# Split products whose moving columns and bank are walked from the last column to the first

## The chip, the core and the metric

The kernel runs on one core of one Trainium2 chip. The metric is the time of one execution on the device in microseconds. Three runs of the kernel before gave 3465.7, 3466.33 and 3469.99 us; the median is 3466.33 us.

## What is computed

The reference is a chain of two transformer blocks over one sequence of 512 positions with 1024 channels, in float32.

- The first block has two layers. Each layer is a gated MLP (`silu(a) * b`, 2816 hidden channels), a mixer, and another gated MLP. The mixer joins sparse attention (compressed, selected and windowed keys, 8 heads) with a gated spatial MLP. Each part has an RMS norm before it, modulated by a condition vector.
- The second block has two layers with a condition vector of its own and a second sequence, the context of 256 positions. Its first layer mixes by pooling, the second by attention over context and latents. Each is followed by an MLP with 4096 hidden channels and a squared ReLU.

Most of the work is in products of the form `x @ W`, with `x` of 512 (or 256) positions:

```
def _swiglu(x, w_in, w_out):
    a, b = jnp.split(x @ w_in, 2, axis=-1)
    return (jax.nn.silu(a) * b) @ w_out
```

## The kernel before

Channels lie on the 128 partitions and positions along the free axis. So an activation tile is `[128, 512]` (128 channels, 512 positions), a half is `[128, 256]`, and the context is `[128, 256]`. A product over 1024 channels is a sum over 8 such tiles.

**The split product.** TensorE is fed with float32 values cut to a shorter format (`F32R`). To keep the accuracy, each weight and each activation is held as a high part and a low part: `WH` and `WL`, `nH` and `nL`, `hH` and `hL`. A product is then three matmuls into the same PSUM bank: high weight by high activation, high weight by low activation, low weight by high activation. The weights are the stationary operand, 128 x 128, and the activations are the moving operand, 512 or 256 columns. These triples are written out in ten places:

- `products` (L662 to L664), which most stages use through `slot_pair`: for each of its `nk` channel tiles it waits for the high and the low part of the activations and issues the triple into one bank.
- `wide_halves_pe` (L1039 to L1041) and `wide_pe` (L1083 to L1085): the same for two to four banks at a time, tile by tile.
- `network_end_pe` (L1299 to L1301), `output_end_pe` (L1345 to L1348), `start_pe` (L1430 to L1432), `second_end_pe` (L2483 to L2485), the blocks at L2562 to L2564, `three` of the context's MLP (L2778 to L2780), and the part of the output projection at L3620 to L3622.

**Weights.** A plan (`plan()`) lists every weight slot in the order of use. SyncE's queue loads a slot of up to 1 MB into a raw buffer, ScalarE rounds it to `WH` (L557), and VectorE subtracts to get `WL` (L568). There are four pairs of `WH` and `WL`; a pair is used again when the last matmul of its slot has counted up a semaphore.

**Readers of the banks.** Each group of matmuls counts up one semaphore with its last instruction. ScalarE or VectorE waits for that count, and then reads the bank: an activation function in the MLPs (L1146), a sum with the residual (L1266, L1277) or with an accumulator (L2454). Eight banks are handed around by `take`.

**Other matmuls.** The attention scores and values (L1737, L1776, L3449, L3477), the transposes (L1756, L3461) and the sums over channels (L877, L882) are plain float32 matmuls, without a split. L3477 is one of them with 512 columns.

The order on each engine is written out by hand; where two stages run beside each other, a helper (`weave`) takes steps of both in turn.

Of the kernel before, what the change touches and what calls it, by code (L numbers as in the profile page):

```python
# [14 lines left out]
KT = 8  # L15
S = 512
# [393 lines left out]
def build(nc, A, out):  # L410
# [3 lines left out]
    with ctx:  # L414
# [234 lines left out]

        def products(pe, k, c, nk, to, xs, ready, group, waits):

            hi, lo = view(M.WH, k), view(M.WL, k)
            cc = slice(c * 128, c * 128 + 128)
            pe.wait_ge(*waits)
            for i in range(nk):
                xh, xl = xs(i)
                (h_hi, v_hi), (h_lo, v_lo) = ready(i)
                pe.wait_ge(h_hi, v_hi)  # L660
                pe.wait_ge(h_lo, v_lo)
                pe.q.matmul(to, hi[:, i, cc], xh, start=i == 0, stop=False)  # L662
                pe.q.matmul(to, hi[:, i, cc], xl, start=False, stop=False)  # L663
                t = pe.q.matmul(to, lo[:, i, cc], xh, start=False, stop=i == nk - 1)  # L664
                if i == nk - 1:
                    t.then_inc(*mm.up(*group))

# [351 lines left out]
        def wide_halves_pe(pe, want, n, g, names):  # L1019

            ks = [slot_pe(pe, want) for _ in range(n)]
            per = slots[ks[0]][5] // 128
            to = []
            for name in names:
                b, free = take(*name)
                pe.wait_ge(*free)
                to.append(b)
            nk = slots[ks[0]][3]
            for x, p in enumerate(lat.half):
                h = g + "AB"[x]  # L1030
                for i in range(nk):
                    pe.wait_ge(*a_xhi.to(h, i))
                    pe.wait_ge(*v_xlo.to(h, i))
                    xh, xl = lat.nH[:, i, p.cols], lat.nL[:, i, p.cols]
                    for j, name in enumerate(names):
                        hi, lo = view(M.WH, ks[j // per]), view(M.WL, ks[j // per])
                        cc = slice(j % per * 128, j % per * 128 + 128)
                        d = to[j][:, p.cols]
                        pe.q.matmul(d, hi[:, i, cc], xh, start=x == i == 0, stop=False, skip_group_check=True)  # L1039
                        pe.q.matmul(d, hi[:, i, cc], xl, start=False, stop=False, skip_group_check=True)  # L1040
                        t = pe.q.matmul(d, lo[:, i, cc], xh, start=False, stop=i == nk - 1, skip_group_check=True)  # L1041
                        if x and i == nk - 1:
                            t.then_inc(*mm.up(*name))
                    if x == 0 and i == 2:
                        half_sum_pe(pe, g + "B", lat.half[1])
                    if x == 0 and i == 4:
                        half_spread_pe(pe, g + "B", lat.half[1])
            for k in ks:
                mm.again("slot", k)
# [15 lines left out]
        def wide_pe(pe, want, n, N, xs, ready, names):  # L1065

            ks = [slot_pe(pe, want) for _ in range(n)]
            per = slots[ks[0]][5] // 128
            to = []
            for name in names:  # L1070
                b, free = take(*name)
                pe.wait_ge(*free)
                to.append(b[:, 0:N])
            nk = slots[ks[0]][3]
            for i in range(nk):
                xh, xl = xs(i)
                (h_hi, v_hi), (h_lo, v_lo) = ready(i)
                pe.wait_ge(h_hi, v_hi)
                pe.wait_ge(h_lo, v_lo)
                for j, name in enumerate(names):  # L1080
                    hi, lo = view(M.WH, ks[j // per]), view(M.WL, ks[j // per])
                    cc = slice(j % per * 128, j % per * 128 + 128)
                    pe.q.matmul(to[j], hi[:, i, cc], xh, start=i == 0, stop=False, skip_group_check=True)  # L1083
                    pe.q.matmul(to[j], hi[:, i, cc], xl, start=False, stop=False, skip_group_check=True)
                    t = pe.q.matmul(to[j], lo[:, i, cc], xh, start=False, stop=i == nk - 1, skip_group_check=True)  # L1085
                    if i == nk - 1:
                        t.then_inc(*mm.up(*name))
            for k in ks:
                mm.again("slot", k)
# [192 lines left out]
        def network_end_pe(g):  # L1282
# [4 lines left out]
            def group(pe, x, o):  # L1287
# [4 lines left out]
                for n, (k, cb, ci, f) in enumerate(parts):  # L1292
                    pe.wait_ge(*a_whi.to(k))
                    pe.wait_ge(*v_wlo.to(k))
                    pe.wait_ge(*a_hhi.to(g, ci, f))
                    pe.wait_ge(*v_hlo.to(g, ci, f))
                    hi, lo = view(M.WH, k)[:, f, 128 * cb:128 * cb + 128], view(M.WL, k)[:, f, 128 * cb:128 * cb + 128]
                    xh, xl = M.hH[:, ci % 2, f, c], M.hL[:, ci % 2, f, c]
                    pe.q.matmul(b[:, 0:S // 2], hi, xh, start=n == 0, stop=False)  # L1299
                    pe.q.matmul(b[:, 0:S // 2], hi, xl, start=False, stop=False)  # L1300
                    t = pe.q.matmul(b[:, 0:S // 2], lo, xh, start=False, stop=n == 5)  # L1301
                t.then_inc(*mm.up(g, "O", x, o))
                if x and o == 3:
                    mm.again("slot", k0)
# [5 lines left out]
        def output_end_pe(g):  # L1310
# [18 lines left out]
            def four(pe):  # L1329
# [6 lines left out]
                for part in (range(6), range(6, 8)):  # L1336
                    for o in range(4):
# [4 lines left out]
                        for i in part:  # L1342
                            pe.wait_ge(*a_hhi.to(g, "m", i))
                            pe.wait_ge(*v_hlo.to(g, "m", i))
                            pe.q.matmul(to[o], hi[:, i, cc], M.mH[:, i, c], start=i == 0, stop=False,  # L1345
                                        skip_group_check=True)
                            pe.q.matmul(to[o], hi[:, i, cc], M.mL[:, i, c], start=False, stop=False, skip_group_check=True)
                            t = pe.q.matmul(to[o], lo[:, i, cc], M.mH[:, i, c], start=False, stop=i == 7,  # L1348
                                            skip_group_check=True)
                        if i == 7:  # L1350
                            t.then_inc(*mm.up(g, "O", 0, o))
# [49 lines left out]
        def start_pe(pe):  # L1401
# [19 lines left out]
            def part(i, which):  # L1421
# [3 lines left out]
                for j in which:  # L1425
# [1 line left out]
                    pe.wait_ge(*a_whi.to(k))  # L1427
                    pe.wait_ge(*v_wlo.to(k))
                    hi, lo = view(M.WH, k), view(M.WL, k)
                    pe.q.matmul(to[j][:, :], hi[:, i, cc], xh, start=i == 0, stop=False, skip_group_check=True)  # L1430
                    pe.q.matmul(to[j][:, :], hi[:, i, cc], xl, start=False, stop=False, skip_group_check=True)
                    t = pe.q.matmul(to[j][:, :], lo[:, i, cc], xh, start=False, stop=i == 7, skip_group_check=True)  # L1432
                    if i == 7:
                        t.then_inc(*mm.up(*names[j]))
                        if j % 2:
# [1031 lines left out]
        def second_end_pe(g):  # L2467
# [4 lines left out]
            def parts(pe, x, o, which, to):  # L2472
                c, cb = lat.half[x].cols, slice(o % 4 * 128, o % 4 * 128 + 128)
                for n in which:
# [3 lines left out]
                    for f in range(4):  # L2478
# [1 line left out]
                        pe.wait_ge(*v_hlo.to(g, ci, f))  # L2480
                        hi, lo = view(M.WH, k)[:, f, cb], view(M.WL, k)[:, f, cb]
                        xh, xl = M.hH2[:, ci % 2, f, c], M.hL2[:, ci % 2, f, c]
                        pe.q.matmul(to, hi, xh, start=n == f == 0, stop=False, skip_group_check=True)  # L2483
                        pe.q.matmul(to, hi, xl, start=False, stop=False, skip_group_check=True)
                        t = pe.q.matmul(to, lo, xh, start=False, stop=n == 1 and f == 3, skip_group_check=True)  # L2485
                if which[-1] == 1:
                    t.then_inc(*mm.up(g, "O", x, o))
                if x and o % 4 == 3 and which[-1] == 1:
# [46 lines left out]
        def after_turn_pe(pe, want, post, g, names, last={}):  # L2535
# [6 lines left out]
            def blocks(x, n, hooks):  # L2542
# [9 lines left out]
                for i in range(KT):  # L2552
# [3 lines left out]
                    for k in n:  # L2556
# [2 lines left out]
                        hi, lo = view(M.WH, k0 + k), view(M.WL, k0 + k)  # L2559
                        for j in range(2):  # L2560
                            cc, d = slice(j * 128, j * 128 + 128), to[2 * k + j][:, c]
                            pe.q.matmul(d, hi[:, i, cc], xh, start=x == i == 0, stop=False, skip_group_check=True)  # L2562
                            pe.q.matmul(d, hi[:, i, cc], xl, start=False, stop=False, skip_group_check=True)
                            t = pe.q.matmul(d, lo[:, i, cc], xh, start=False, stop=i == KT - 1, skip_group_check=True)  # L2564
                            if x and i == KT - 1:
                                t.then_inc(*mm.up(*names[2 * k + j]))
                        if x and i == KT - 1:
# [197 lines left out]
        def context_on_pe(pe):  # L2765
# [9 lines left out]

            def three(to, k, i, cc, xh, xl, start, stop):
                hi, lo = view(M.WH, k), view(M.WL, k)
                pe.q.matmul(to, hi[:, i, cc], xh, start=start, stop=False, skip_group_check=True)  # L2778
                pe.q.matmul(to, hi[:, i, cc], xl, start=False, stop=False, skip_group_check=True)  # L2779
                return pe.q.matmul(to, lo[:, i, cc], xh, start=False, stop=stop, skip_group_check=True)  # L2780

            def first(ci, f):

# [823 lines left out]
        def merge_end_pe():  # L3607
# [4 lines left out]
            def part(pe, x, o, tiles, to):  # L3612
# [4 lines left out]
                for i in tiles:  # L3617
                    pe.wait_ge(*a_yhi.to("y2", i))
                    pe.wait_ge(*v_ylo.to("y2", i))
                    pe.q.matmul(to, hi[:, i, cc], lat.nH[:, i, c], start=i == 0, stop=False, skip_group_check=True)  # L3620
                    pe.q.matmul(to, hi[:, i, cc], lat.nL[:, i, c], start=False, stop=False, skip_group_check=True)
                    t = pe.q.matmul(to, lo[:, i, cc], lat.nH[:, i, c], start=False, stop=i == 7, skip_group_check=True)  # L3622
                if tiles[-1] == 7:
                    t.then_inc(*mm.up("wo", "O", x, o))
                    if x and o % 2:
# [321 lines left out]
```

## Time and profile before

| what | before |
|---|---|
| median of 3 runs | 3466.33 us |
| span of the profiled execution, first to last instruction | 3464.7 us |
| TensorE matmul busy | 3413.6 us (99%), 18494 matmuls |
| TensorE weight load busy | 2874.5 us (83%) |
| VectorE busy | 2165.7 us (63%) |
| ScalarE busy | 1318.4 us (38%) |
| mean granted TensorE clock | 0.997 |
| HBM traffic | 130 GB/s over the span |

The profiled execution has no time of its own beside its span; the timed runs lie 1.0 to 5.3 us above it. A matmul's row in the trace lasts longer than the step from its start to the next one's start, because matmuls are pipelined: 390 ns against about 227 ns for 512 columns. So the pace of TensorE is read from the starts in the time line, and the busy share from how little idle time is left.

### The profile page before, as it was taken

What the parts mean: (1) busy time and instruction counts of PE and PEld (TensorE: products, weight loads), DVE (VectorE), ACT (ScalarE), POOL (GpSimd) and SP (SyncE); (2) the same over time, 40 slices, a digit from 0 to 9 for tenths busy, and PEclk for the clock granted to TensorE, in tenths of its full rate; (3) what the DMA queues carried; (4) which work ended last, traced back from release to release, by engine and by line L of the source; (5) the groups of instructions that cost most, each with busy time, mean ns of one, the idle gap of its engine ahead of it and who ended that gap; (6) DMA issues with size and microseconds to landing.
All of it is one profiled execution on the core that took longest, in us unless ns stands there. A gap on an engine that the chain in (4) does not pass through costs nothing.

```text
span 3464.7 us, 46915 instructions
## 1 busy us (share of the span) xinstructions
PE 3413.6 (99%) x18494; PEld 2874.5 (83%) x18494; DVE 2165.7 (63%) x3570; ACT 1318.4 (38%) x1951; POOL 298.0 (9%) x376
## 2 busy tenths in 40 slices
PE   9999999999999999999999999999999999999998
PEld 7888967898888988896789888899988898588888
DVE  7555565656555655666577777888776556655444
ACT  4222463333222422245333523355533236643222
POOL 0000232001000100023100000012100001210000
PEclk9999999999999999999999999999999999999999
DMA  7444302434444344320243444344444311013221
GB/s 279 188 158 163 107 24 101 163 129 168 158 162 151 134 169 158 148 106 12 101 164 140 149 150 170 146 147 182 172 174 165 117 66 68 25 50 112 96 98 48
DMA packets 85561, 452.01 MB, mean 130 GB/s; under 512 B 10304, under 2 KB 12544, under 8 KB 48608
## 3 DMA queue, kind: packets, MB, share of 16 engines
q1 hardware_dynamic: 83168, 439.10, 34.2%
q0 software_dynamic: 2176, 9.92, 0.8%
q8 instruction: 148, 2.42, 0.3%
q14 instruction: 69, 0.57, 0.0%
HBM read 446.88 MB, written 2.10 MB: 130 GB/s over the span
## 4 chain that ended last, share of the span: by engine, by line
PE 84%; DVE 7%; ACT 3%; issue 2%; DMA 2%; POOL 0%; SPq 0%; DVEq 0%; ACTq 0%; POOLq 0%
PE ps L662 21%; PE ps L663 21%; PE ps L664 21%; DVE WL L568 2%; DMA araw<-in_ast 2%; PE ps L2778 1%; PE ps L2780 1%; PE ps L2779 1%; PE ps L3477 1%; PE ps L1039 1%; PE ps L1040 1%; PE ps L1041 1%; ACT P L1859 1%; PE ps L1776 1%; PE ps L1299 1%
## 5 line engine op out<-in xcount | busy, mean ns | idle before, releaser
L662 PE MATMUL ps<-nH,WH 128*128 128x512 f32 x2256 | 880.3, 390 | 0.4 <-ACT rot L3207 0.4
L664 PE MATMUL ps<-nH,WL 128*128 128x512 f32 x2256 | 877.8, 389 | 0.0
L663 PE MATMUL ps<-nL,WH 128*128 128x512 f32 x2256 | 877.8, 389 | 0.0
L568 DVE TENSOR_TENSOR WL<-raw,WH 128x2048 fp32r<-128x2048 f32 (+2 forms) x297 | 651.6, 2199 | 361.5 <-ACT WH L557 360.0
L557 ACT ACTIVATE WH<-raw 128x2048 fp32r<-128x2048 f32 (+2 forms) x299 | 543.2, 1822 | 561.1 <-PE ps L664 479.9
L662 PEld LDWEIGHTS ps<-nH,WH 128*128 128x128 f32 x2256 | 423.5, 188 | 90.6 <-issue 3.3
L664 PEld LDWEIGHTS ps<-nH,WL 128*128 128x128 f32 x2256 | 423.4, 188 | 88.3
L663 PEld LDWEIGHTS ps<-nL,WH 128*128 128x128 f32 x2256 | 423.5, 188 | 87.2 <-issue 0.2
L628 DVE SCALAR_TENSOR_TENSOR araw<-araw,cB 128x1024 f32<-128x1024 f32 x224 | 275.6, 1230 | 205.6 <-DMA araw<-in_ast 205.2
L662 PE MATMUL ps<-hH,WH 128*128 128x512 f32 x944 | 368.8, 391 | 2.5 <-DVE ma L2454 1.4
L664 PE MATMUL ps<-hH,WL 128*128 128x512 f32 x944 | 367.4, 389 | 0.0
L663 PE MATMUL ps<-hL,WH 128*128 128x512 f32 x944 | 367.2, 389 | 0.0
L1146 ACT ACTIVATE scr<-ps 128x512 f32<-128x512 f32 x152 | 89.5, 595 | 414.4 <-PE ps L664 387.2
L1012 POOL TENSOR_SCALAR scr<-scr,der,mods 128x256 f32<-128x256 f32 x112 | 86.2, 771 | 1805.8 <-DVE scr L925 1804.8
L1153 ACT ACTIVATE hH<-scr 128x512 fp32r<-128x512 f32 x152 | 95.8, 633 | 357.5 <-DVE scr L1199 355.5
L662 PEld LDWEIGHTS ps<-hH,WH 128*128 128x128 f32 x944 | 177.2, 188 | 40.3 <-DVE ma L2454 1.9
L664 PEld LDWEIGHTS ps<-hH,WL 128*128 128x128 f32 x944 | 177.2, 188 | 36.9
L663 PEld LDWEIGHTS ps<-hL,WH 128*128 128x128 f32 x944 | 177.2, 188 | 36.6
L1199 DVE TENSOR_TENSOR scr<-scr,ps 128x512 f32<-128x512 f32 x88 | 59.5, 687 | 108.4 <-PE ps L664 107.0
L1266 DVE SCALAR_TENSOR_TENSOR h<-ps,der,h 128x512 f32<-128x512 f32 x144 | 99.7, 746 | 27.2 <-PE ps L664 25.9
L1202 DVE TENSOR_TENSOR scr<-scr 128x512 f32<-128x512 f32 x64 | 43.1, 690 | 101.3 <-ACT scr L1146 100.9
L1208 DVE TENSOR_TENSOR hL<-scr,hH 128x512 fp32r<-128x512 f32 x152 | 100.8, 687 | 4.3
(452 smaller groups left out, 5940.0 us busy)
## 6 DMA issues: line engine op xcount, KB each, us to landing
raw<-in_wst SPq DMA_DIRECT2D x273, 1024.0 KB, 4.8
araw<-in_ast SPq DMA_DIRECT2D x225, 512.0 KB, 5.7
raw<-in_wst SPq DMA_DIRECT2D x18, 512.0 KB, 3.3
araw<-in_wst SPq DMA_DIRECT2D x9, 1024.0 KB, 4.8
row<-in_ast SPq DMA_DIRECT2D x15, 512.0 KB, 10.5
cw<-in_cw POOLq DMA_DIRECT2D x4, 1024.0 KB, 5.9
h<-in_xT SPq DMA_DIRECT2D x4, 512.0 KB, 5.6
raw<-in_wst SPq DMA_DIRECT2D x8, 256.0 KB, 2.6
```

The source lines that it names most:

```text
L557: act.q.activation(M.WH[k % NW][:, 0:n], M.raw[raw_use[k]][:, 0:n], ACT.Copy).then_inc(*a_whi.up(k))
L568: dve.q.tensor_tensor(M.WL[k % NW][:, 0:n], M.raw[raw_use[k]][:, 0:n], M.WH[k % NW][:, 0:n].bitcast(F32), ALU.subtract).then_inc(*v_wlo.up(k))
L628: dve.q.scalar_tensor_tensor(out=w[:, :], in0=w[:, :], scalar=1.0, in1=M.cB[q][:, :], op0=ALU.mult, op1=ALU.mult, accum_out=total).then_in ...
L662: pe.q.matmul(to, hi[:, i, cc], xh, start=i == 0, stop=False)
L663: pe.q.matmul(to, hi[:, i, cc], xl, start=False, stop=False)
L664: t = pe.q.matmul(to, lo[:, i, cc], xh, start=False, stop=i == nk - 1)
L1012: pool.q.tensor_scalar(p.scr[2 + i % 2][:, p.cols], p.scr[i % 2][:, p.cols], G[:, i:i + 1], shift[:, i:i + 1], ALU.mult, ALU.add).then_inc ...
L1146: act.q.activation(p.scr[n % 2][:, 0:N], bank(g, "a", ci, f)[:, 0:N], ACT.Silu if gated else ACT.Relu).then_inc(*empties(a_fn, g, "a", ci, f))
L1153: act.q.activation(hH[:, ci % 2, f, :], p.scr[(2 if gated else 0) + f % 2][:, 0:N], ACT.Copy if gated else ACT.Square).then_inc(*a_hhi.up( ...
L1199: dve.q.tensor_tensor(p.scr[2 + u][:, 0:N], p.scr[u][:, 0:N], bank(g, "b", ci, f)[:, 0:N], ALU.mult).then_inc(*empties(v_pr, g, "b", ci, f))
L1208: dve.q.tensor_tensor(hL[:, ci % 2, f, :], p.scr[2 + f % 2][:, 0:N], hH[:, ci % 2, f, :].bitcast(F32), ALU.subtract).then_inc(*v_hlo.up(g, ...
L1266: dve.q.scalar_tensor_tensor(out=M.h[:, o, :], in0=bank(g, "o", ci, o)[:, :], scalar=gate[:, o:o + 1], in1=M.h[:, o, :], op0=ALU.mult, op1 ...
```

## The change

A helper `back(a)` returns `a[:, ::-1]`, the same columns in reverse order. In all ten places, each of the three matmuls of a triple gets its output and its moving operand through `back`. The weights stay as they are. Each column is still multiplied by the same weights and lands in the same place of the bank; the instruction starts with the last column and ends with the first. The other matmuls are not touched, and neither is anything on the other engines. The diff, cut to the helper, the first two places and the context's:

```diff
@@ -649,6 +649,10 @@
 
 
 
+        def back(a):
+
+            return a[:, ::-1]
+
         def products(pe, k, c, nk, to, xs, ready, group, waits):
 
             hi, lo = view(M.WH, k), view(M.WL, k)
@@ -659,9 +663,9 @@
                 (h_hi, v_hi), (h_lo, v_lo) = ready(i)
                 pe.wait_ge(h_hi, v_hi)
                 pe.wait_ge(h_lo, v_lo)
-                pe.q.matmul(to, hi[:, i, cc], xh, start=i == 0, stop=False)
-                pe.q.matmul(to, hi[:, i, cc], xl, start=False, stop=False)
-                t = pe.q.matmul(to, lo[:, i, cc], xh, start=False, stop=i == nk - 1)
+                pe.q.matmul(back(to), hi[:, i, cc], back(xh), start=i == 0, stop=False)
+                pe.q.matmul(back(to), hi[:, i, cc], back(xl), start=False, stop=False)
+                t = pe.q.matmul(back(to), lo[:, i, cc], back(xh), start=False, stop=i == nk - 1)
                 if i == nk - 1:
                     t.then_inc(*mm.up(*group))
 
@@ -1036,9 +1040,9 @@
                         hi, lo = view(M.WH, ks[j // per]), view(M.WL, ks[j // per])
                         cc = slice(j % per * 128, j % per * 128 + 128)
                         d = to[j][:, p.cols]
-                        pe.q.matmul(d, hi[:, i, cc], xh, start=x == i == 0, stop=False, skip_group_check=True)
-                        pe.q.matmul(d, hi[:, i, cc], xl, start=False, stop=False, skip_group_check=True)
-                        t = pe.q.matmul(d, lo[:, i, cc], xh, start=False, stop=i == nk - 1, skip_group_check=True)
+                        pe.q.matmul(back(d), hi[:, i, cc], back(xh), start=x == i == 0, stop=False, skip_group_check=True)
+                        pe.q.matmul(back(d), hi[:, i, cc], back(xl), start=False, stop=False, skip_group_check=True)
+                        t = pe.q.matmul(back(d), lo[:, i, cc], back(xh), start=False, stop=i == nk - 1, skip_group_check=True)
                         if x and i == nk - 1:
                             t.then_inc(*mm.up(*name))
                     if x == 0 and i == 2:
...
@@ -2775,9 +2779,9 @@
 
             def three(to, k, i, cc, xh, xl, start, stop):
                 hi, lo = view(M.WH, k), view(M.WL, k)
-                pe.q.matmul(to, hi[:, i, cc], xh, start=start, stop=False, skip_group_check=True)
-                pe.q.matmul(to, hi[:, i, cc], xl, start=False, stop=False, skip_group_check=True)
-                return pe.q.matmul(to, lo[:, i, cc], xh, start=False, stop=stop, skip_group_check=True)
+                pe.q.matmul(back(to), hi[:, i, cc], back(xh), start=start, stop=False, skip_group_check=True)
+                pe.q.matmul(back(to), hi[:, i, cc], back(xl), start=False, stop=False, skip_group_check=True)
+                return pe.q.matmul(back(to), lo[:, i, cc], back(xh), start=False, stop=stop, skip_group_check=True)
 
             def first(ci, f):
 
...
```

The places left out have the same three lines with the same edit.

## Rows read from the trace of the kernel before

**Rows 1.** The page: its head, TensorE's busy time, and the granted clock in 40 slices.
```profile
span 3464.7 us, 46915 instructions
...
PE 3413.6 (99%) x18494; PEld 2874.5 (83%) x18494; DVE 2165.7 (63%) x3570; ACT 1318.4 (38%) x1951; POOL 298.0 (9%) x376
...
PEclk9999999999999999999999999999999999999999
```

**Rows 2.** The page: chain that ended last, by engine and by line.
```profile
PE 84%; DVE 7%; ACT 3%; issue 2%; DMA 2%; POOL 0%; SPq 0%; DVEq 0%; ACTq 0%; POOLq 0%
PE ps L662 21%; PE ps L663 21%; PE ps L664 21%; DVE WL L568 2%; DMA araw<-in_ast 2%; PE ps L2778 1%; PE ps L2780 1%; PE ps L2779 1%; PE ps L3477 1%; PE ps L1039 1%; PE ps L1040 1%; PE ps L1041 1%; ACT P L1859 1%; PE ps L1776 1%; PE ps L1299 1%
```

**Rows 3.** Waits of TensorE: line, awaited engine and line, us in total, times, longest.
```profile
PE ps L1756 <- ACT P L1859: 9.0, 25, 0.5
```

**Rows 4.** Groups by form: line, tiles, shapes, count | busy us, mean ns | idle before; 512 columns.
```profile
L662 PE MATMUL ps<-nH,WH 128*128 128x512 f32 x2256 | 880.3, 390 | 0.4 <-ACT rot L3207 0.4
...
L662 PE MATMUL ps<-hH,WH 128*128 128x512 f32 x944 | 368.8, 391 | 2.5 <-DVE ma L2454 1.4 <-DVE h L1266 1.1
...
L662 PE MATMUL ps<-yaH,WH 128*128 128x512 f32 x64 | 24.9, 389 | 0.0
...
L1430 PE MATMUL ps<-nH,WH 128*128 128x512 f32 x48 | 19.0, 397 | 2.4 <-DVE WL L568 1.4 <-DVE nL L1524 0.8 <-PE ps L682 0.2
...
L1083 PE MATMUL ps<-nH,WH 128*128 128x512 f32 x16 | 6.2, 389 | 0.0
```

**Rows 5.** The same view, 256 columns, first line of each triple.
```profile
L1039 PE MATMUL ps<-nH,WH 128*128 128x256 f32 x320 | 92.1, 288 | 0.3
...
L1299 PE MATMUL ps<-hH,WH 128*128 128x256 f32 x288 | 82.7, 287 | 1.0 <-DVE hL L1208 0.6
...
L2483 PE MATMUL ps<-hH,WH 128*128 128x256 f32 x256 | 73.2, 286 | 0.0
...
L2562 PE MATMUL ps<-nH,WH 128*128 128x256 f32 x192 | 57.1, 297 | 3.2 <-DVE nL L930 1.9 <-DVE WL L580 1.1
...
L3620 PE MATMUL ps<-nH,WH 128*128 128x256 f32 x128 | 37.3, 291 | 0.0
...
L1345 PE MATMUL ps<-mH,WH 128*128 128x256 f32 x64 | 18.1, 283 | 0.0
...
L662 PE MATMUL ps<-nHk,WH 128*128 128x256 f32 x32 | 8.9, 279 | 0.0
...
L662 PE MATMUL ps<-nHc,WH 128*128 128x256 f32 x16 | 4.5, 281 | 0.0
```

**Rows 6.** Time line of TensorE, 24 starts apart: start us, duration us, line; 512 columns.
```profile
1000.25 0.39 PE L662 MATMUL ps<-hH,WH 128*128 128x512 f32 x1
...
1005.69 0.39 PE L662 MATMUL ps<-hH,WH 128*128 128x512 f32 x1
```

**Rows 7.** Time line of TensorE, 27 starts apart; 256 columns.
```profile
3417.22 0.28 PE L2484 MATMUL ps<-hL,WH 128*128 128x256 f32 x1
...
3420.46 0.28 PE L2484 MATMUL ps<-hL,WH 128*128 128x256 f32 x1
```

**Rows 8.** Time line of TensorE in the context's MLP, 12 starts apart.
```profile
2381.88 0.28 PE L2778 MATMUL ps<-hHc,WH 128*128 128x256 f32 x1
...
2383.24 0.28 PE L2778 MATMUL ps<-hHc,WH 128*128 128x256 f32 x1
```

**Rows 9.** Time line of TensorE two starts apart, and the window's busy times, clock.
```profile
2865.61 0.41 PE L2564 MATMUL ps<-nH,WL 128*128 128x256 f32 x1
...
2866.04 0.41 PE L2563 MATMUL ps<-nL,WH 128*128 128x256 f32 x1
...
2865.00:2868.00 3.00, 2.98 (x12) 2.80 (x13) 0.97 (x5) 0.00 (x0) 0.00 (x0) 0.50 0.56 194
```

**Rows 10.** Chain in order of time: start us, duration us, what.
```profile
2947.52 5.15 PE ps L3477 x12
```

**Rows 11.** Window from 2300 to 2400 us: busy times in the page's order of engines.
```profile
2300.00:2400.00 100.00, 99.16 (x791) 95.76 (x791) 91.03 (x106) 58.38 (x68) 28.03 (x20) 1.00 0.47 172
```

More of the change, by code:

```diff
@@ L1082, in wide_pe @@
                     cc = slice(j % per * 128, j % per * 128 + 128)
-                    pe.q.matmul(to[j], hi[:, i, cc], xh, start=i == 0, stop=False, skip_group_check=True)
-                    pe.q.matmul(to[j], hi[:, i, cc], xl, start=False, stop=False, skip_group_check=True)
-                    t = pe.q.matmul(to[j], lo[:, i, cc], xh, start=False, stop=i == nk - 1, skip_group_check=True)
+                    pe.q.matmul(back(to[j]), hi[:, i, cc], back(xh), start=i == 0, stop=False, skip_group_check=True)
+                    pe.q.matmul(back(to[j]), hi[:, i, cc], back(xl), start=False, stop=False, skip_group_check=True)
+                    t = pe.q.matmul(back(to[j]), lo[:, i, cc], back(xh), start=False, stop=i == nk - 1, skip_group_check=True)
                     if i == nk - 1:
@@ L1298, in group @@
                     xh, xl = M.hH[:, ci % 2, f, c], M.hL[:, ci % 2, f, c]
-                    pe.q.matmul(b[:, 0:S // 2], hi, xh, start=n == 0, stop=False)
-                    pe.q.matmul(b[:, 0:S // 2], hi, xl, start=False, stop=False)
-                    t = pe.q.matmul(b[:, 0:S // 2], lo, xh, start=False, stop=n == 5)
+                    pe.q.matmul(back(b[:, 0:S // 2]), hi, back(xh), start=n == 0, stop=False)
+                    pe.q.matmul(back(b[:, 0:S // 2]), hi, back(xl), start=False, stop=False)
+                    t = pe.q.matmul(back(b[:, 0:S // 2]), lo, back(xh), start=False, stop=n == 5)
                 t.then_inc(*mm.up(g, "O", x, o))
@@ L1344, in four @@
                             pe.wait_ge(*v_hlo.to(g, "m", i))
-                            pe.q.matmul(to[o], hi[:, i, cc], M.mH[:, i, c], start=i == 0, stop=False,
+                            pe.q.matmul(back(to[o]), hi[:, i, cc], back(M.mH[:, i, c]), start=i == 0, stop=False,
                                         skip_group_check=True)
-                            pe.q.matmul(to[o], hi[:, i, cc], M.mL[:, i, c], start=False, stop=False, skip_group_check=True)
-                            t = pe.q.matmul(to[o], lo[:, i, cc], M.mH[:, i, c], start=False, stop=i == 7,
+                            pe.q.matmul(back(to[o]), hi[:, i, cc], back(M.mL[:, i, c]), start=False, stop=False, skip_group_check=True)
+                            t = pe.q.matmul(back(to[o]), lo[:, i, cc], back(M.mH[:, i, c]), start=False, stop=i == 7,
                                             skip_group_check=True)
@@ L1429, in part @@
                     hi, lo = view(M.WH, k), view(M.WL, k)
-                    pe.q.matmul(to[j][:, :], hi[:, i, cc], xh, start=i == 0, stop=False, skip_group_check=True)
-                    pe.q.matmul(to[j][:, :], hi[:, i, cc], xl, start=False, stop=False, skip_group_check=True)
-                    t = pe.q.matmul(to[j][:, :], lo[:, i, cc], xh, start=False, stop=i == 7, skip_group_check=True)
+                    pe.q.matmul(back(to[j][:, :]), hi[:, i, cc], back(xh), start=i == 0, stop=False, skip_group_check=True)
+                    pe.q.matmul(back(to[j][:, :]), hi[:, i, cc], back(xl), start=False, stop=False, skip_group_check=True)
+                    t = pe.q.matmul(back(to[j][:, :]), lo[:, i, cc], back(xh), start=False, stop=i == 7, skip_group_check=True)
                     if i == 7:
@@ L2482, in parts @@
                         xh, xl = M.hH2[:, ci % 2, f, c], M.hL2[:, ci % 2, f, c]
-                        pe.q.matmul(to, hi, xh, start=n == f == 0, stop=False, skip_group_check=True)
-                        pe.q.matmul(to, hi, xl, start=False, stop=False, skip_group_check=True)
-                        t = pe.q.matmul(to, lo, xh, start=False, stop=n == 1 and f == 3, skip_group_check=True)
+                        pe.q.matmul(back(to), hi, back(xh), start=n == f == 0, stop=False, skip_group_check=True)
+                        pe.q.matmul(back(to), hi, back(xl), start=False, stop=False, skip_group_check=True)
+                        t = pe.q.matmul(back(to), lo, back(xh), start=False, stop=n == 1 and f == 3, skip_group_check=True)
                 if which[-1] == 1:
@@ L2561, in blocks @@
                             cc, d = slice(j * 128, j * 128 + 128), to[2 * k + j][:, c]
-                            pe.q.matmul(d, hi[:, i, cc], xh, start=x == i == 0, stop=False, skip_group_check=True)
-                            pe.q.matmul(d, hi[:, i, cc], xl, start=False, stop=False, skip_group_check=True)
-                            t = pe.q.matmul(d, lo[:, i, cc], xh, start=False, stop=i == KT - 1, skip_group_check=True)
+                            pe.q.matmul(back(d), hi[:, i, cc], back(xh), start=x == i == 0, stop=False, skip_group_check=True)
+                            pe.q.matmul(back(d), hi[:, i, cc], back(xl), start=False, stop=False, skip_group_check=True)
+                            t = pe.q.matmul(back(d), lo[:, i, cc], back(xh), start=False, stop=i == KT - 1, skip_group_check=True)
                             if x and i == KT - 1:
@@ L3619, in part @@
                     pe.wait_ge(*v_ylo.to("y2", i))
-                    pe.q.matmul(to, hi[:, i, cc], lat.nH[:, i, c], start=i == 0, stop=False, skip_group_check=True)
-                    pe.q.matmul(to, hi[:, i, cc], lat.nL[:, i, c], start=False, stop=False, skip_group_check=True)
-                    t = pe.q.matmul(to, lo[:, i, cc], lat.nH[:, i, c], start=False, stop=i == 7, skip_group_check=True)
+                    pe.q.matmul(back(to), hi[:, i, cc], back(lat.nH[:, i, c]), start=i == 0, stop=False, skip_group_check=True)
+                    pe.q.matmul(back(to), hi[:, i, cc], back(lat.nL[:, i, c]), start=False, stop=False, skip_group_check=True)
+                    t = pe.q.matmul(back(to), lo[:, i, cc], back(lat.nH[:, i, c]), start=False, stop=i == 7, skip_group_check=True)
                 if tiles[-1] == 7:
```

## The prediction

> **What bounds the kernel now.** The head of the profile page comes first: the reader is to see a TensorE that is busy for 3413.6 of 3464.7 us, under a granted clock of nine tenths or more in every slice [rows 1]. A busy matmul row says little of pace, though, since each row lasts about 390 ns while the next one starts much earlier. So the second view is the chain of waits by engine and line: 84% of it lies on TensorE, and the three lines of `products` alone make 63% (21% each) [rows 2]. Third, the table of waits: the longest sum of idle time that any producer causes before a matmul line is 9.0 us, and it belongs to transposes that the change leaves alone [rows 3]. The kernel is bound by how fast TensorE takes one matmul after another, and the only question is what this change does to that pace.
>
> The pace stands in the time line. In a run of 512-column split products the starts go from 1000.25 to 1005.69 us over 24 steps, 0.2267 us each [rows 6]. In a run of 256-column ones they go from 3417.22 to 3420.46 us over 27 steps, 0.1200 us each [rows 7]. The difference, 106.7 ns for 256 columns, is 0.4167 ns a column, one column per cycle of the 2.4 GHz level at which the clock stands there. What is left is the same for both widths: 226.7 - 213.3 = 13.3 ns and 120.0 - 106.7 = 13.3 ns, a fixed term for each matmul. A split product therefore costs 0.4167 ns times its columns plus 13.3 ns, and the change can act on either part.
>
> **How many there are.** The 512-column groups come in threes of equal count: 2256 + 944 + 2 x 64 + 48 + 2 x 16 = 3408 triples, or 10,224 matmuls (the rows with 64 and 16 each stand for two groups) [rows 4]. The 256-column ones: 320 + 288 + 3 x 256 + 2 x 192 + 128 + 64 + 32 + 16 = 2000 triples, or 6,000 matmuls (256 stands for three groups, 192 for two) [rows 5]. At the paces above these are 10,224 x 0.2267 = 2318 us and 6,000 x 0.1200 = 720 us, together 3038 us, 88% of the span. All 16,224 are changed, out of 18,494.
>
> **The change part by part.**
>
> *Instructions, waits, queues.* Nothing is added or removed: `back` makes a view, and each matmul keeps its weights, its waits, its place in the order and its increment. The helper writes the same columns to the same places, only in the other order. No DMA is moved, and no wait is added on any engine. Cost 0.
>
> *The readers of the banks and of the moving tiles.* ScalarE and VectorE wait for the increment of the last matmul of a group, not for single columns. The column that is written last is now column 0 instead of 511, and neither end is read earlier. Cost 0. The weight loads stay as they are, with 128 columns read forwards, and they run beside the matmul before. Cost 0.
>
> *Reading the moving columns backwards.* The time line has no matmul that reads with a negative step, so its price has to be bounded. The step keeps its size of one element; the address falls instead of rising. From below: nothing can go faster than one column per cycle, so the column part cannot shrink, and only the fixed term can: at most 13.3 x 16,224 = 216 us. The nearest row of a shorter one is a stretch of context products in which the starts go from 2381.88 to 2383.24 us over 12 steps, 113.3 ns each, 6.7 ns less than usual for 256 columns [rows 8]. From above: the stream falls to half its pace. Two rows show what that costs. The float32 matmuls of L3477 take 5.15 us for 12, 429 ns for 512 columns [rows 10]. In the one stretch where the granted clock is 0.50 (the 1.2 GHz level; TensorE had sat idle before it), 256-column split products start at 2865.61 and 2866.04, two steps in 0.43 us, 215 ns each [rows 9]. I take 0: the nearest rows are those of the same instruction with a step of the same size, and nothing in them suggests that 0.4167 ns a column depends on whether addresses rise.
>
> *Writing the bank backwards.* The same bounds, since one stream feeds the other. Every output slice here has 256 or 512 columns and starts at an even column, so the backward walk starts at an odd one (511, or 255), and it takes neighbours in the same pairs as the forward walk (511 with 510, instead of 510 with 511). If the memory takes columns by twos, no pair is torn. I take 0 again.
>
> Here the Trainium skill has a rule that speaks against the change. The row shows full pace at rising addresses, 0.4167 ns a column [rows 6, 7]; no row shows falling ones. In the Trainium skill, "Advanced Engine Details and Errata", section "PSUM Cachelines", PSUM has lines of 8 bytes, two float32 values, and any access pattern that isn't contiguous slows matmuls down significantly, since every two consecutive elements should be contiguous. By a strict reading, a falling pattern isn't contiguous and the first rival below holds; by the reason that the section gives, each two consecutive elements still share one such line and the cost is 0. I hold with the reason, and no row here decides it.
>
> *Sum.* 0 + 0 + 0 + 0 = 0 against the profiled execution's span of 3464.7 us. The median of the timed runs is 3466.33 us, 1.6 us above that span; the forecast is **3466.3 us**.
>
> **Rivals.**
>
> *A: the stream falls to half pace (slower).* Place: the two-column step at the read or at the bank write. If hardware merges two columns into one access only when addresses rise, each column takes its own, and the matmul goes at the pace of rows 9 and 10. Price: 10,224 x (0.429 - 0.2267) = 2068 us and 6,000 x (0.215 - 0.120) = 570 us, so 3466 + 2638 = about **6100 us**. For it speaks that the float32 matmuls of the same width go at just that pace [rows 10], so a slower mode of the stream exists and a column isn't bound to 0.4167 ns. Against it: in those the slower pace goes with the number format, not with an order of columns. It decides as soon as one of the two sides can't merge falling pairs.
>
> *B: the fixed term gets longer (slower).* Place: the seam between two matmuls, where the reader now has to begin at the far end of a row, and the first columns come later. If the seam is paid twice, the price is another 13.3 ns x 16,224 = 216 us, **3682 us**; each nanosecond is 16.2 us, and it shows from 0.43 ns a matmul. For it: a fixed term exists at full clock and is not explained by the column count [rows 6, 7]. Against it: it is the same for 256 and 512 columns, so it looks like a property of the switch and not of where a row begins.
>
> *C: the fixed term gets shorter (faster).* The same seam in the other direction. The row at 113.3 ns shows that 6.7 ns of it can go, without any change in the instructions [rows 8]. If all split products went that way: 6.7 x 16,224 = 108 us, **3358 us**. What is late next is then VectorE, which is busy for 91% of the stretch from 2300 to 2400 us [rows 11]; there the gain would stop at about 9 of 100 us. Elsewhere TensorE has room, as it waits for almost nothing [rows 3]. Against it: that row is a stretch in which reading order was the usual one, so something else brings it about.
>
> *D: the change doesn't do what it says.* The addresses could be put in rising order again on the way to the instruction. Then nothing changes: 3466 us, the same as the forecast, told apart only by the pattern of the instructions.
>
> **How the numbers follow.** Forecast (no change in pace) 0.64, D 0.02, A 0.11, B 0.11, C 0.12. A change of 0.2% (7 us, 0.43 ns a matmul) is about what a measurement of this kernel can tell from none. So faster 0.12, same 0.66, slower 0.22. The forecast's own range is 3460 to 3473 us. A is so far off that it can't be held in a range of use, and with its 0.11 left out, the range takes about half of B and of C: from 3440 (1.6 ns less a matmul: 16.2 x 1.6 = 26) to 3520 us (3.3 ns more a matmul: 54). About 0.11 + 0.05 + 0.05 lies outside.
>
> **What would show it.** In the profile after, the starts in a run of 512-column split products should be 226 to 227 ns apart and those of 256-column ones 120 ns; the mean durations in the groups should stay at 389 to 391 and 280 to 288 ns [rows 4, 5], TensorE's busy time near 3413 us and the granted clock full. 429 and 215 ns would be rival A. A shift that is the same number of nanoseconds for both widths would be B or C; a shift that doubles from 256 to 512 columns would be a change of the stream's pace, and would prove the argument from rows 6 and 7 wrong. If the pace stands and the time still moves, the cause lies in the readers of the banks, which I have put at 0.

## The result: 1.65% slower

Three runs of the changed kernel gave 3523.08, 3524.57 and 3524.7 us, against 3465.7 to 3469.99 us before. The ratio is 1.0165, with a 95% interval of 1.0147 to 1.0183: slower by 58 us. The forecast was 3466.3 us, no change, with a range up to 3520 us; the time lies above it.

The head of the page of the changed kernel, its chain by engine and by line, and the longest wait, which answer to [rows 1 to 3]. The lines of `products` have moved from L662 to L666, because of the new helper.

```profile
span 3522.8 us, 46915 instructions
...
PE 3476.8 (99%) x18494; PEld 2875.3 (82%) x18494; DVE 2167.6 (62%) x3570; ACT 1317.1 (37%) x1951; POOL 297.0 (8%) x376
...
PEclk9999999999999999999999999999999999999999
...
PE 89%; DVE 5%; ACT 3%; issue 1%; DMA 0%; POOL 0%; DVEq 0%; SPq 0%; ACTq 0%; POOLq 0%
```

```profile
PE ps L1760 <- ACT P L1863: 9.2, 26, 0.5
```

The other engines do what they did: VectorE 2167.6 us against 2165.7, ScalarE 1317.1 against 1318.4, the same wait of 9 us, the same clock. TensorE alone is busy for longer, by 63.2 us, and its share of the chain went from 84 to 89%. So the time went into the matmuls.

Which of them is seen in the groups by form (line, tiles, shapes, count, then busy us and mean ns), against [rows 4, 5]:

```profile
L666 PE MATMUL ps<-nH,WH 128*128 128x512 f32 x2256 | 898.7, 398 | 0.4 <-ACT rot L3211 0.4
...
L666 PE MATMUL ps<-hH,WH 128*128 128x512 f32 x944 | 376.3, 399 | 0.7 <-DVE h L1270 0.7
...
L1043 PE MATMUL ps<-nH,WH 128*128 128x256 f32 x320 | 91.7, 286 | 0.5 <-issue 0.2
...
L2487 PE MATMUL ps<-hH,WH 128*128 128x256 f32 x256 | 72.9, 285 | 0.0
```

With 512 columns a matmul's row became 8 ns longer (390 to 398, 391 to 399); with 256 columns it became 1 to 2 ns shorter. The pace is again in the starts of the time line: 24 steps apart at 512 columns and 30 steps apart at 256.

```profile
1005.05 0.40 PE L666 MATMUL ps<-nH,WH 128*128 128x512 f32 x1
...
1010.65 0.40 PE L666 MATMUL ps<-nH,WH 128*128 128x512 f32 x1
```

```profile
3474.78 0.28 PE L2488 MATMUL ps<-hL,WH 128*128 128x256 f32 x1
...
3478.32 0.28 PE L2488 MATMUL ps<-hL,WH 128*128 128x256 f32 x1
```

That is 5.60 / 24 = 233.3 ns against 226.7 [rows 6], and 3.54 / 30 = 118.0 ns (118.3 from the unrounded starts) against 120.0 [rows 7]. The steps at 256 columns are no longer even: they run 115 to 123 ns in a pattern. At 10,224 matmuls, 6.67 ns would make 68 us. Summed over every step from one start to the next, which takes in the waits, the 512-column split products grew by 63.0 us (2330.8 to 2393.8), those of 256 columns fell by 3.1 us (737.3 to 734.2), and all others by 1.6 us. Together that is 58.3 us, against 58.1 in the span.

### The profile page after: what moved, and what is told of

It reads as the page before. It is cut to its first block, busy times and chain, and to the rows that moved or that the text cites. A ratio compares the mean times of both kernels' runs of the same rounds, so it can differ in the third digit from the quotient of the medians.

```text
span 3522.8 us, 46915 instructions
## 1 busy us (share of the span) xinstructions
PE 3476.8 (99%) x18494; PEld 2875.3 (82%) x18494; DVE 2167.6 (62%) x3570; ACT 1317.1 (37%) x1951; POOL 297.0 (8%) x376
## 4 chain that ended last, share of the span: by engine, by line
PE 89%; DVE 5%; ACT 3%; issue 1%; DMA 0%; POOL 0%; DVEq 0%; SPq 0%; ACTq 0%; POOLq 0%
PE ps L666 22%; PE ps L667 22%; PE ps L668 22%; PE ps L2782 2%; PE ps L2784 2%; PE ps L2783 2%; PE ps L3481 1%; ACT P L1863 1%; PE ps L1043 1%; PE ps L1044 1%; PE ps L1045 1%; PE ps L1780 1%; PE ps L1303 1%; PE ps L1304 1%; PE ps L1305 1%
## 5 line engine op out<-in xcount | busy, mean ns | idle before, releaser
L666 PE MATMUL ps<-nH,WH 128*128 128x512 f32 x2256 | 898.7, 398 | 0.4 <-ACT rot L3211 0.4
L667 PE MATMUL ps<-nL,WH 128*128 128x512 f32 x2256 | 896.5, 397 | 0.0
L668 PE MATMUL ps<-nH,WL 128*128 128x512 f32 x2256 | 896.5, 397 | 0.0
L666 PEld LDWEIGHTS ps<-nH,WH 128*128 128x128 f32 x2256 | 424.2, 188 | 104.3 <-issue 3.3
L666 PE MATMUL ps<-hH,WH 128*128 128x512 f32 x944 | 376.3, 399 | 0.7 <-DVE h L1270 0.7
L667 PE MATMUL ps<-hL,WH 128*128 128x512 f32 x944 | 375.1, 397 | 0.0
L668 PE MATMUL ps<-hH,WL 128*128 128x512 f32 x944 | 375.1, 397 | 0.0
L666 PEld LDWEIGHTS ps<-hH,WH 128*128 128x128 f32 x944 | 177.5, 188 | 43.6 <-DVE h L1270 1.1
```

Source lines behind the costliest of these rows:

```text
L666: pe.q.matmul(back(to), hi[:, i, cc], back(xh), start=i == 0, stop=False)
L667: pe.q.matmul(back(to), hi[:, i, cc], back(xl), start=False, stop=False)
L668: t = pe.q.matmul(back(to), lo[:, i, cc], back(xh), start=False, stop=i == nk - 1)
```

## The experiments

**Read or write (e1, e2), and the width (e3).** The helper was split in two, `back` for the moving operand and `back_out` for the output. In e1 `back` returns `a[:, ::-1]` and `back_out` returns `a`, so only the moving operand is turned round. In e2 it is the other way about. In e3 both are turned round, but only where there are 256 columns. Against the kernel before, cut to one matmul and to e3's helpers:

```diff
-                pe.q.matmul(to, hi[:, i, cc], xh, start=i == 0, stop=False)
+                pe.q.matmul(back_out(to), hi[:, i, cc], back(xh), start=i == 0, stop=False)
...
+        def back(a):
+
+            return a[:, ::-1] if a.shape[1] == S // 2 else a
+
+        def back_out(a):
+
+            return a[:, ::-1] if a.shape[1] == S // 2 else a
```

> All ten places read their moving columns backwards and write the bank forwards, so the columns of every split product land in reverse order (the output is not the reference's). Theory 1 (the read): about 3524 us, as the changed kernel, and 233 ns a 512-column matmul. Theory 2 (the write): about 3466 us and 227 ns.

> All ten places read forwards and write the bank backwards (the output is not the reference's). Theory 1 (the read): about 3466 us and 227 ns. Theory 2 (the write): about 3524 us and 233 ns. If each half costs something, both lie between.

> Only the products of 256 columns (6,000 matmuls) are walked backwards, read and write; those of 512 columns go forwards as before. In the changed kernel the 256-column starts came in a pattern of 115 to 123 ns with a mean near 118.5 in place of 120. Theory 'the term depends on the width': 512-column matmuls at 227 ns, 256-column ones at about 118.5, so 6000 x 1.2 ns = 7 us less than before, about 3459 us. Theory 'the seam costs the same for each': about 6000/16224 of the 58 us lost, 3488 us.

| kernel | median us | ratio to before | 95% interval |
|---|---|---|---|
| e1, read backwards | 3524.18 | 1.0169 | 1.0154 to 1.0184 |
| e2, write backwards | 3465.42 | 0.9998 | 0.9989 to 1.0008 |
| e3, both, 256 columns only | 3459.68 | 0.9984 | 0.9975 to 0.9993 |

The time line of e1 and then that of e2, 24 steps apart each:

```profile
1004.71 0.40 PE L672 MATMUL ps<-nH,WL 128*128 128x512 f32 x1
...
1010.31 0.40 PE L672 MATMUL ps<-nH,WL 128*128 128x512 f32 x1
```

```profile
999.75 0.39 PE L671 MATMUL ps<-nL,WH 128*128 128x512 f32 x1
...
1005.19 0.39 PE L671 MATMUL ps<-hL,WH 128*128 128x512 f32 x1
```

Reading backwards alone gives 233.3 ns and the whole loss. Writing backwards alone gives 226.7 ns and no loss. e3 came out as its first theory said (3459 expected, 3459.68 measured): 256 columns gain a little, and that version is faster than the kernel before by 0.16%. (The 118.5 ns that it was expected to show had been read from the changed kernel.)

**The pace by itself (m1).** A small kernel keeps activations and weights resident and lets TensorE run alone, with one stretch of 48 matmuls for each variant. It ran once, with the granted clock at 1.00 in every stretch.

> A small kernel in place of the whole computation (its output is not the reference's): TensorE alone runs stretches of 48 split-product matmuls on resident tiles, one source line per stretch, with the moving columns, the bank's columns, both or neither walked backwards, for 512, 448, 384, 320 and 256 columns, with the weights taken 4 to 128 columns further on, with 96, 64 or 32 weight columns in place of 128, and in bf16 and plain float32. Theory 1 (the moving read, falling beside a weight load, loses time to it): read-only costs 233.3 ns at 512 columns as both do, write-only stays at 226.7; the fixed term shrinks with the number of weight columns (64 columns: about half of 13.3 ns forward and of 20 ns backward), and shifting the weights changes it. Theory 2 (the bank's write in falling order costs at the seam): write-only costs 233.3, read-only 226.7, and the number of weight columns changes nothing. Either way the plain float32 form should stay at 429 ns, since it runs at half the pace.

One triple of it, as it stands when both operands are turned round (`q` is put here for the shift of the weights, which each stretch has as a number; the triple stands on one line there):

```
mm(back(banks[b][:, 0:512]), hi[:, i, q:q+128], back(nH[:, i, 0:512]), start=i == 0, stop=False)
mm(back(banks[b][:, 0:512]), hi[:, i, q:q+128], back(nL[:, i, 0:512]), start=False, stop=False)
mm(back(banks[b][:, 0:512]), lo[:, i, q:q+128], back(nH[:, i, 0:512]), start=False, stop=i == 7)
```

Its time line, always 24 steps apart: L69 forwards, L71 read backwards, L73 written backwards, L109 forwards with the weights 16 columns on, L117 forwards with them 64 columns on.

```profile
40.71 0.39 PE L69 MATMUL ps<-nH,WL 128*128 128x512 f32 x1
...
46.15 0.39 PE L69 MATMUL ps<-nH,WL 128*128 128x512 f32 x1
...
51.63 0.40 PE L71 MATMUL ps<-nH,WL 128*128 128x512 f32 x1
...
57.23 0.40 PE L71 MATMUL ps<-nH,WL 128*128 128x512 f32 x1
...
62.81 0.39 PE L73 MATMUL ps<-nH,WL 128*128 128x512 f32 x1
...
68.25 0.39 PE L73 MATMUL ps<-nH,WL 128*128 128x512 f32 x1
...
225.18 0.39 PE L109 MATMUL ps<-nH,WL 128*128 128x512 f32 x1
...
230.78 0.39 PE L109 MATMUL ps<-nH,WL 128*128 128x512 f32 x1
...
270.24 0.39 PE L117 MATMUL ps<-nH,WL 128*128 128x512 f32 x1
...
275.68 0.39 PE L117 MATMUL ps<-nH,WL 128*128 128x512 f32 x1
```

In order: 226.7, 233.3, 226.7, 233.3 and 226.7 ns. The first three repeat the large kernel with TensorE alone, so no other engine and no DMA has a part in it. The fourth is the surprise: nothing in it is turned round, the moving columns and the bank are those of L69, only the weights begin 64 bytes further on, and the loss is the same. At 256 bytes it is gone. The means of the steps in the other stretches:

```
columns        forwards   read and written backwards
512            226.7      233.3
448            202.8      206.7
384            173.3      177.8
320            146.7      146.7
256            119.8      118.3
512, only the third matmul of each triple backwards      228.8
512, only the second                                     229.1
512, weights 4, 8, 16, 32 columns on     forwards 233.4, 233.2, 233.4, 232.6; backwards 233.3, 233.3, 233.3, 240.0
512, weights 64, 128 columns on          forwards 226.9, 226.7; backwards 233.3, 233.3
512, 96, 64, 32 weight columns           forwards 230.0, 229.8, 231.7; backwards 233.3 each
512, bf16                                215.8       215.8
512, float32, per row of the trace       429.2       429.2
```

So what I had called a fixed term is none. Forwards at the first place it is 13.1 to 13.3 ns at four of the five widths and 16.1 at 448 columns, but backwards it is 20.0 at 512 and 448, 17.8 at 384, 13.3 at 320 and 11.6 at 256. It depends on the width, on the direction of the read and on where the weights lie. With one matmul in three turned round, about a third of the loss is paid (2.1 and 2.4 of 6.7 ns), so it belongs to each matmul and not to a change of direction. bf16 and plain float32 show no dependence on the direction. (Plain float32 leaves two rows for each matmul, 96 for the 48 of its stretch, so one of its matmuls of 512 columns takes 858 ns.) Theory 1 was right on the read, and wrong where it expected the term to shrink with the number of weight columns: with 32 of them it is no smaller.

**Where the two tiles lie (m2).** The starts of the moving tile and of the weights were stepped together, in one run of a second small kernel.

> A small kernel in place of the whole computation (its output is not the reference's): stretches of 42 split-product matmuls, TensorE alone, one source line each. The first small kernel showed that the term beyond one column per cycle is not fixed: with the weights taken 4, 8, 16 or 32 columns further on, forward reading costs 233 ns too, at 64 and 128 columns it is back at 226.7, and backward reading with 32 columns costs 240. Here the starting column of the moving tile (0 to 56) and that of the weights (0 to 48) are stepped together in both reading directions, and 256 columns in a coarser grid. Theory 'address phase' (the moving stream and the weight load meet in the same parts of SBUF, as a matter of their addresses modulo 64 columns, 256 bytes): the pace depends on the difference of the two starts, for backward reading some pair of starts gives 226.7 or less, and another gives 240. Theory 'direction' (falling addresses cost 6.7 ns whatever the place): the backward stretches lie at or above 233.3 at every start.

Mean step in ns at 512 columns, as worked out from the starts; `w` is the start of the weights in their tile, the head line the start of the moving columns:

```
             0      8      16     24     32     40     48     56
forwards
w 0        226.7  233.3  228.8  233.7  233.3  234.3  233.3  233.3
w 16       233.3  233.2  226.7  233.3  228.8  233.7  233.3  234.3
w 32       232.2  234.4  233.3  233.3  226.9  233.3  228.8  233.7
w 48       229.0  233.4  233.3  234.3  233.3  233.3  226.9  233.3
backwards
all 32     233.3 in each
```

Two places of the forward table: the moving tile at 48 and the weights at 0 (L81, 233.3 ns), and both at 16 (L89, 226.7 ns), 24 steps apart:

```profile
99.72 0.39 PE L81 MATMUL ps<-nH,WH 128*128 128x512 f32 x1
...
105.32 0.39 PE L81 MATMUL ps<-nH,WH 128*128 128x512 f32 x1
...
138.87 0.39 PE L89 MATMUL ps<-nH,WH 128*128 128x512 f32 x1
...
144.31 0.39 PE L89 MATMUL ps<-nH,WH 128*128 128x512 f32 x1
```

The forward table has its good places on a diagonal: 226.7 to 226.9 ns where moving columns and weights start at the same place modulo 64 columns (256 bytes), 228.8 to 229.0 where the moving columns are 16 ahead, and 232 to 234.4 everywhere else. The good place is narrow: with the weights 2 or 6 columns on, further stretches took 230.7 and 230.0 ns. Reading backwards takes 233.3 ns at all 32 pairs. The theory 'address phase' holds for the forward direction alone. What 'direction' says of the backward stretches came true, but not that only the direction costs, since most forward places cost the same 6.7 ns. The loss of the change is thus the loss of a good place. One limit: every start tried was an even column, so a backward read always began at an odd one, and whether it has a good place at the shifts between is not shown. 256 columns in the same kernel took 119.9 ns at equal starts, and between 113.7 and 118.8 at unequal ones; backwards between 117.7 and 120.0.

**The same in the large kernel (e4, e5, e6).** A pad at the right end of SBUF sets where the normed and most hidden activations lie. It was made 16 columns wider for a forward (e4) and a backward kernel (e5), and 16 narrower for a forward one (e6).

```diff
-    sb(ctx, "pad", [128, 24], side="right")
+    sb(ctx, "pad", [128, 40], side="right")      # e4 on the kernel before, e5 on the changed one
+    sb(ctx, "pad", [128, 8], side="right")       # e6 on the kernel before
```

> The kernel before, all products forwards, with the pad at the right end of SBUF widened from 24 to 40 float32 columns, so that the normed and most of the hidden activations lie 16 columns (64 bytes) lower against the weights; nothing else changes. Theory 'address phase': the 512-column pace goes from 226.7 to 233.3 ns for these tiles, as the second small kernel has it for a moving start 48 columns ahead of the weights, and the 256-column one from 120 to between 113.7 and 118; with at most 10,224 x 6.7 = 68 us lost and some 5,000 x 2 to 6 = 10 to 30 us won, 3500 to 3525 us. Theory 'direction alone': 3466 us, since nothing is read backwards.

> The changed kernel with the same wider pad. In the second small kernel, backward reading took 233.3 ns at every start of the moving tile. Theory 'address phase' in that form: 512 columns stay at 233.3 ns, 256 columns move between 117.7 and 120, so 3515 to 3530 us, and the gap to the forward kernel with the same pad is small. Theory 'direction costs 6.7 ns on top of the phase': 240 ns, about 3590 us.

> The kernel before, forwards, with the pad narrowed from 24 to 8 columns: these tiles lie 16 columns higher against the weights. The second small kernel has 228.8 ns at 512 columns and 117.8 at 256 for this phase. If its table carries over, up to 10,224 x 2.1 = 21 us are lost and some 5,000 x 2.2 = 11 us won: about 3476 us, between 3468 and 3488. Theory 'direction alone': 3466 us.

| kernel | median us | ratio to before | 95% interval | mean step of 512-column `nH`, `nL` |
|---|---|---|---|---|
| e4, forwards, pad 40 | 3508.51 | 1.0123 | 1.0108 to 1.0138 | 233.3 ns |
| e5, backwards, pad 40 | 3522.65 | 1.0164 | 1.0149 to 1.0179 | 233.3 ns |
| e6, forwards, pad 8 | 3479.93 | 1.0040 | 1.0026 to 1.0054 | 229.0 ns |

The time line of e4, 24 steps apart, where nothing is read backwards (5.60 us, 233.3 ns):

```profile
999.80 0.39 PE L664 MATMUL ps<-nH,WL 128*128 128x512 f32 x1
...
1005.40 0.39 PE L664 MATMUL ps<-nH,WL 128*128 128x512 f32 x1
```

The steps are averaged without those that hold a wait (over 260 ns). All three times came out inside what the address phase gave. The forward kernel with its tiles 64 bytes lower loses 42 us with no column turned round, the backward kernel doesn't mind the move, and at 16 columns higher the 228.8 ns of the small kernel return as 229.0. The addresses that the program gives its tiles fit too. In the kernel before, both tiles of all 10,224 matmuls of 512 columns start 128 bytes past a multiple of 256, so all are level. The wider pad moves the moving tile of 8,664 of them, which then take 233.3 ns, and leaves 1,560 level, which take 227.2. So e4 loses less than the change, and its 256-column products gained: over all steps 737.3 to 723.5 us.

## Why the prediction was wrong, point by point

- **What bounds the kernel, and how many matmuls there are: right.** Over all 512-column steps without a wait the mean went from 226.8 to 233.3 ns, which makes 67 us for the 10,224 matmuls of [rows 4]. Waits in such steps fell by 4 us (11.8 to 8.1), the 256-column steps by 3 us and the other matmuls by 1.6 us, which leaves 58 us. (DMA and VectorE had 9% of the chain before and have 5% after.)
- **Instructions, waits, queues, readers of the banks: cost 0, right.** The busy times of the other engines stand, and e2 is at 0.9998.
- **Writing the bank backwards: cost 0, right.** e2 shows it, with 226.7 ns. Here the rule that spoke against the change was weighed: the bank's falling order gave no loss, so the strict reading of the Trainium skill ("Advanced Engine Details and Errata", section "PSUM Cachelines", any pattern that isn't contiguous slows matmuls down) does not hold for it. The section's other sentence, that every two consecutive elements should be contiguous, agrees with the run; that lines of two values are the reason is not shown.
- **Reading the moving columns backwards: taken as 0, the step that failed.** It measured 6.7 ns a matmul at 512 columns and about -1 to -2 ns at 256. My ground was that the nearest rows were the same instruction with a step of the same size. They were, but at a single place: all 512-column matmuls of the kernel before have tiles that start level with their weights, and I took for a property of the instruction what m2 shows to be one of that place.
- **The fixed term: misread.** From 226.7 - 213.3 = 13.3 and 120.0 - 106.7 = 13.3 ns I concluded a term that belongs to the switch between matmuls. Both rows came from level tiles, where the term is indeed nearly the same at four of five widths (m1). Elsewhere it isn't: m1 has 20.0 and 11.6 ns backwards, and m2 has 13.3 to 21 forwards at 512 columns. The warning stood in the trace, as the 113.3 ns of [rows 8], and I set it aside as "something else". Those are products of the context, whose tiles start 64 bytes lower against the weights (16 columns behind, which is 48 ahead modulo 64). m2 has 113.7 and 117.8 ns for the two pairs of starts in that relation.
- **"The weight loads stay as they are ... Cost 0": incomplete.** They run beside the matmul before, and their place against the moving tile sets the forward pace. Moving the weights alone by 64 bytes costs 6.7 ns (L109 of m1). The Trainium skill, "TensorE: Matmul & The Clock Gate", section "Step-by-step: what each phase is for", has two independent read ports in SBUF and no read bandwidth lost to the next weights. For bf16 the runs don't speak against it (215.8 ns whichever way the columns are read; other places of the weights were not tried); for the split products they do as far as the place of the weights changes the pace of the running matmuls; that read bandwidth is what is lost is not shown.
- **Rivals.** A (half pace, 6100 us) did not come, on either side. B (the term gets longer) had the right sign, with 6.7 ns in place of its 13.3, but not the right mechanism: a seam would cost the same at every width, and 320 columns lost nothing while 512 lost 6.7. C (shorter) came at 256 columns, small. D (nothing changes) falls with the changed pace. Of the two signs that were named, a shift equal at both widths or one that doubles, neither came: it was +6.7 ns at 512 columns and -1.5 at 256. I gave both slower cases 0.22 together and cut the range where half of B began; the width of the term's own spread in the trace, 6.6 to 13.3 ns, should have made it wider.
- **Two misreadings that change no sum.** The 12 rows of L3477 are 6 matmuls, since plain float32 leaves two rows for each (96 rows for 48 matmuls); 429 ns is the price of a row, and rival A's ground, float32 matmuls at just half the pace, is off by two. And the stretch of [rows 9] isn't the only one at 0.50: the granted clock is also 0.50 from 1591.6 to 1595.0 us, and for about 7 us near the start.

**What stays open.** Why a backward read was in a good place at none of the starts tried is not shown; neither is why the place of the weights changes the pace, nor why fewer weight columns don't help. One pair measured differently in the two small kernels: weights 32 columns on and read backwards took 240.0 ns with 8 tiles (m1) and 233.3 with 7 (m2). And 256-column steps have more than one steady value at the same relation of starts: in the kernel before, the context's steps have a mean of 117.4 ns and stretches of 113.3 [rows 8].

## What to carry to other kernels

When TensorE's pace exceeds one column per cycle by a constant, do not book the rest as overhead of the instruction until it has been seen at a second address: for `F32R` matmuls at full pace, shift the weights by 64 bytes against the moving tile and look at the starts again. Let both begin at the same place modulo 256 bytes for forward reads of 512 columns (at 256 columns that was the slowest place), and treat every new allocation or pad as a change to the matmuls. A walk order that looks free on paper deserves one small kernel with one stretch per variant, which here told read from write in a single run.

## What the runs showed that I had not expected

- The forward pace at 512 columns moves between 226.7 and 234.4 ns with the addresses alone, and the whole kernel with it: 3466 us (level), 3480 us (moving tiles 16 columns up) and 3509 us (16 columns down).
- The bank can be written in falling order at no cost (0.9998, interval 0.9989 to 1.0008).
- At 256 columns level tiles are the worst place forwards (119.9 ns against 113.7 to 118.8). Turning these products alone round pays there: in e3 the level ones went from 119.9 to 118.4 ns, and the context's, which aren't level, from 117.4 to 117.8. It takes 3459.68 us. Its rows below are 30 steps apart (3.55 us, 118.3 ns).

```profile
3409.75 0.28 PE L2491 MATMUL ps<-hH,WH 128*128 128x256 f32 x1
...
3413.30 0.28 PE L2491 MATMUL ps<-hH,WH 128*128 128x256 f32 x1
```
